# Another table of preferences for the list planner of an attention stage

## The reference

```
s_c = einsum(q, kc);  o_c = softmax(s_c) @ vc        # compressed keys, one for 16 tokens
idx = top_k(score from p_c, 16)                       # blocks of 64 keys to select
o_s = softmax(q @ ks[idx]) @ vs[idx]                  # selected blocks
o_w = softmax(q @ kw, window 512) @ vw                # sliding window
o   = g0 * o_c + g1 * o_s + g2 * o_w
x   = layer_norm(alpha * x + concat(A, o * silu(b_gate)) @ w_out)
```

## Time and profile before

| | |
|---|---|
| median of 3 runs | 1091.5 us (1091.16 to 1092.84) |
| the profiled execution, its own time | 1080.46 us |
| its span, from the first instruction to the last | 1078.6 us |
| TensorE busy, of the span | 96% |
| DVE, ACT, POOL busy, of the span | 70%, 34%, 34% |
| mean granted clock of TensorE | 0.994 of full speed |
| attention on TensorE | 383.8 to 656.8 us |

### The profile page before, as it was taken

The page is one execution under the profiler, slowest core; times in us unless marked ns, Lnnn a source line. Parts: engine busy times, 40 slices in busy tenths (PEclk is TensorE's granted clock), DMA queues, the critical chain, the costliest instruction groups (busy, mean ns, idle before and its releaser), DMA issues.

```text
span 1078.6 us, 19288 instructions
## 1 busy us (share of the span) xinstructions
PE 1034.3 (96%) x7764; PEld 881.2 (82%) x7764; DVE 757.2 (70%) x1397; ACT 371.5 (34%) x785; POOL 369.5 (34%) x384
## 2 busy tenths in 40 slices
PE   6999999999999989999999999999999999999997
PEld 5888999999998965556655666887999999998875
DVE  4577889999898978977678665657546710267755
ACT  3211111122223467878666864111112211253000
POOL 3544540000010498675785562100122211317000
PEclk9999999999999999999999999999999999999999
DMA  8645332144312025040673078312221111042321
GB/s 240 214 166 183 106 115 60 37 163 123 114 40 44 1 90 157 24 137 2 213 258 119 2 238 237 131 64 83 69 88 39 53 44 47 1 156 79 137 83 63
DMA packets 85889, 113.75 MB, mean 105 GB/s; under 512 B 21952, under 2 KB 67144, under 8 KB 85727
## 3 DMA queue, kind: packets, MB, share of 16 engines
q1 hardware_dynamic: 71849, 69.51, 21.2%
q0 software_dynamic: 11776, 41.95, 11.5%
q10 hardware_dynamic: 2182, 1.16, 0.4%
HBM read 100.91 MB, written 16.64 MB: 109 GB/s over the span
## 4 chain that ended last, share of the span: by engine, by line
PE 80%; DVE 6%; POOL 5%; DMA 3%; issue 3%; ACT 1%; SPq 0%; DVEq 0%; POOLq 0%
PE PS L758 25%; PE PS L2165 16%; PE PS L1933 14%; PE PS L1283 4%; PE PS L1395 4%; PE PS L1265 4%; PE PS L746 3%; PE PS L1957 2%; DMA WRAW<-in_w_in_even 2%; POOL RING L1659 2%; PE PS L1946 1%; DVE ACC L597 1%; DMA RING<-in_cache_kv_sel,idx 1%; PE PS L2145 1%; POOL PRW L1674 1%
## 5 line engine op out<-in xcount | busy, mean ns | idle before, releaser
L644 DVE SCALAR_TENSOR_TENSOR Y<-U,SM,Y 128x1024 f32<-128x1024 f32 x120 | 150.1, 1314 | 0.3
L758 PE MATMUL PS<-XH,WH 128*128 128x352 f32 (+1 forms) x624 | 141.3, 330 | 0.0
L758 PE MATMUL PS<-XL,WH 128*128 128x352 f32 (+1 forms) x624 | 138.9, 327 | 0.0
L758 PE MATMUL PS<-XH,WL 128*128 128x352 f32 (+1 forms) x624 | 138.0, 325 | 0.0
L2272 POOL TENSOR_TENSOR WL<-WRAW,WH 128x1024 fp32r<-128x1024 f32 x14 | 37.5, 2675 | 212.8 <-ACT WH L2217 212.8
L758 PEld LDWEIGHTS PS<-XH,WH 128*128 128x128 f32 (+1 forms) x624 | 103.6, 185 | 2.4
L758 PEld LDWEIGHTS PS<-XH,WL 128*128 128x128 f32 (+1 forms) x624 | 104.1, 185 | 1.4
L758 PEld LDWEIGHTS PS<-XL,WH 128*128 128x128 f32 (+1 forms) x624 | 103.8, 185 | 1.4
L597 DVE SCALAR_TENSOR_TENSOR ACC<-PS,SM,ACC 128x508 f32<-128x508 f32 x124 | 86.9, 742 | 25.1 <-PE PS L746 23.1
L2165 PE MATMUL PS<-XH,WH 128*128 128x352 f32 x360 | 77.2, 323 | 0.0
L2165 PE MATMUL PS<-XH,WL 128*128 128x352 f32 x360 | 77.1, 323 | 0.0
(11 more groups left out here) (354 smaller groups left out, 1991.4 us busy)
## 6 DMA issues: line engine op xcount, KB each, us to landing
WRAW<-in_w_in_even SPq DMA_DIRECT2D x16, 512.0 KB, 3.8
WRAW<-in_w_in_odd SPq DMA_DIRECT2D x16, 512.0 KB, 4.0
TM<-in_state_win_kv SPq DMA_DIRECT2D x12, 512.0 KB, 6.8
XIN<-in_x_prompt SPq DMA_DIRECT2D x8, 512.0 KB, 15.6
WRAW<-in_w_in_even SPq DMA_DIRECT2D x16, 256.0 KB, 3.7
XR<-in_x_prompt SPq DMA_DIRECT2D x8, 512.0 KB, 3.5
layer_out<-R SPq DMA_DIRECT2D x8, 512.0 KB, 2.6
XR<-layer_out SPq DMA_DIRECT2D x8, 512.0 KB, 3.3
```

The source lines that it names most:

```text
L644: v.scalar_tensor_tensor(dst, src, CWT[:, i, t:t + 1], dst, ALU.mult, ALU.add).then_inc(s_cv, 1)
L758: ins = pe.matmul(PS[0:mcols, 3 * slot + c, 0:CH], w[:, slot, kk, 0:mcols], x[:, kk, c * CH:(c + 1) * CH], start=(kk == 0 and n == 0), sto ...
```

## The change

Two tables of numbers are replaced. The steps, their lengths, the waits and the rule of choice stay as they are, and so do all instructions; what can differ is the order in which each engine gets its steps, and by it when SP's and POOL's transfers start. The numbers are ns and compare with `remains`, which is at most 193800 and falls to the step's own length at the end of the stage.

```diff
--- before.py
+++ after.py
@@ -1189,13 +1189,12 @@
         assert len(remains) == len(about)
 
 
-        PREFER = {("ACT", "E"): -23000, ("ACT", "P"): 53000, ("ACT", "X"): -28000, ("DVE", "M"): -28000, ("DVE", "O"):
-                  -69000, ("DVE", "P"): 465000, ("DVE", "X"): -164000, ("PE", "D"): 118000, ("PE", "T"): 2000, ("PE", "V"):
-                  -114000, ("PE", "X"): -67000, ("POOL", "C"): 134000}
-        PREFER_EIGHTH = {("ACT", "E", 2): -12000, ("ACT", "E", 3): -31000, ("DVE", "R", 1): 43000, ("PE", "D", 0):
-                  -54000, ("PE", "K", 3): 143000, ("PE", "K", 4): 15000, ("PE", "K", 7): -3000, ("PE", "S", 0): 70000, ("PE", "S",
-                  4): 15000, ("PE", "S", 6): -19000, ("PE", "S", 7): -8000, ("PE", "T", 2): 44000, ("PE", "T", 3): 5000, ("PE",
-                  "T", 4): 17000}
+        PREFER = {("ACT", "E"): 23000, ("ACT", "P"): 176000, ("ACT", "W"): 46000, ("DVE", "H"): -128000, ("DVE", "M"):
+                  -47000, ("DVE", "P"): 601000, ("DVE", "X"): -310000, ("PE", "D"): 113000, ("PE", "K"): -1000, ("PE", "S"):
+                  -39000, ("PE", "V"): -280000, ("PE", "X"): -43000}
+        PREFER_EIGHTH = {("ACT", "E", 1): 68000, ("DVE", "M", 2): -27000, ("DVE", "O", 1): 19000, ("PE", "D", 0):
+                  -115000, ("PE", "K", 1): -108000, ("PE", "K", 3): 112000, ("PE", "K", 4): 19000, ("PE", "S", 0): 109000, ("PE",
+                  "S", 3): -90000, ("PE", "S", 4): 97000, ("PE", "T", 4): 18000, ("PE", "T", 7): -63000}
         order = {e: [] for e in todo}
         now, end, turned_last, pe_mode = dict.fromkeys(todo, 0), {}, [None], WHOLE
         lines = {(e, k): len(todo[e][k]) for e in todo for k in todo[e]}
```

## The result

The changed kernel takes **1096.6 us** (median of 8 runs, 1093.32 to 1099.48) against 1090.81 of the kernel before beside it (8 runs, 1089.71 to 1092.84): ratio 1.0047, interval [1.0033, 1.0062] (5.1 us by the ratio, 5.8 by the medians). The forecast was 1088.5, faster, with a range up to 1095.3. So the sign is wrong and the time lies outside the range. The profiled execution took 1097.15 us, its span is 1095.3 us.

The account below looks back on a forecast made before the run. TensorE bounds the kernel, busy 1034.3 of 1078.6 us, with 17.4 us of gaps in attention. Tail -2.4, clock -1.6 and later scalings +1.0 sum to -3.0: 1088.5 us from 1091.5, 8-in-10 range 1084.8 to 1095.3.

Parts of the forecast that it names:

- Behind attention nothing gives it back: Output projection after attention: 34.4 us of solid matmul cover the second half's weights, so attention's saving reaches the end.
- the 49: Choices, of 1297 along the old order, that the new table changes: 14 ACT, 13 DVE, 11 TensorE, 11 POOL.
- the rivals I set against the forecast: POOL starves the turns 16%, 1095.5; turns beside turns 12%, 1094.1; DMA bounds the tail 27%, 1090.9; orders hardly differ 3%, 1091.5.
- The DMA rival: Transfers fill the DMA engines in attention's tail: landings move only 0.64 us, gap and lower clock stay; 1090.9 us, 27%.
- The sign that I had named for it: Sign of DMA as the tail's bound: the last gather still lands 26 us behind the window loads' issue.
- The tail, -2.4: End of attention: earlier samples' values parts bring gathers forward, cutting 3.07 us of TensorE stalls to 0.7; -2.4 us.
- The clock, -1.6: Near 650 us: without a gap near 2 us TensorE's stay at the lower clock goes; -1.6 us, bounds 0 and 1.6.
- The sign for the tail: Gap ahead of the last values part under 1 us, and no granted clock under 0.95 around it.
- The start, 0: Ten early ACT choices, copies ahead of exponentials: POOL's queue is full, so worth 0; bounds -4.8 to +0.6 us.
- The sign that I had named for the start: The gap of about 3 us on POOL's scaling near 402 is still there.
- The middle, 0: TensorE's swapped turns and key turns: 0, or 2.6 us either way; sign: gaps sum to 4 to 7 us.
- The base: The 11.0 us between profiled 1080.46 and scored median 1091.5, carried over unchanged to turn 1077.5 into 1088.5.

Follow-up runs that it names:

- old_order: The kernel before, unchanged, run again for a second trace on the chip of the first kernels tested: 1090.46 us, ratio 1.0001.
- new_order: The changed kernel, unchanged, measured again beside the kernel before: 1095.2 us, ratio 1.0046.
- new_y_last: The changed kernel with output-projection tiles Y0 and Y1 put back behind the last output turn and V79: 1089.17 us, 0.9984 of the kernel before.
- pv_apart: Changed kernel, Y0 and Y1 behind V79, a values step V between samples' values parts 1 and 2 in both halves: 1088.03 us, 0.9987 of the kernel before.
- y_split: Changed kernel with Y0 ahead of the last output turn and V79, and Y1 behind them: 1087.44 us, 0.9988 of the kernel before, second chip.
- old_y_first: The kernel before with only Y0 and Y1 moved ahead of the last output turn and V79: 1095.88 us, ratio 1.0048.
- the first four experiments: Both kernels unchanged, the changed one with Y0 and Y1 behind V79, the one before with them ahead; one chip: 1090.46, 1095.2, 1089.17, 1095.88 us.
- start_act: The kernel before with only ACT's new preferences for the first 28 of 80 turns, both Y tiles at the end: 1075.79 us, ratio 0.9983.
- the cut at the 54th turn: New table until 54 of 80 turns are placed, old table behind, both Y tiles at the end: 1074.46 us, 0.9963 of the kernel before.

## Why the prediction was wrong

**"Behind attention nothing gives it back"** is the step that failed, and it is worth more than all the others: the whole +5.6. I read 34.4 us of solid matmul in the earlier trace rows as a property of that stretch. It was a property of the order: TensorE was solid there because two tiles stood between the last O and the first weights that wait for O. The planner's code says what would move them. Y waits for the weight step `("wol", 3)`, and behind V79 and O the planner sees nothing: V79 has 1564 ns of work behind it, Y0 has 11080. Run through the planner's loop, the old table ends `wol` 3 at 256.8 us of its own clock, in the moment V79 ends. The new one ends it at 253.0, just before V79's turn at 253.4, so Y wins. It would win under the old preference for V, too (1564 - 114000 is also below 11080). The weights wait for values part 4, which ends 3.5 us earlier by that clock, while TensorE comes to V79's place only 2.6 us earlier. So the earlier samples' parts, which I forecast as the gain, are themselves what let Y pass V79. The planner books that as a success: its last TensorE step ends at 265.6 instead of 268.0, while its last O goes from 257.6 to 266.3. The join behind O is in neither number, as no step of the planner stands there.

**Comparing choices along the old order** hid it. I counted 49 of 1297 choices, and held the rest to be drift. In the end 145 of 333 positions on TensorE differ. Even of the 49 the prediction priced only a part: eight of the eleven on POOL, gathers ahead of the scalings C65 to C77 in the middle, have no term in it. A list scheduler's table can be run in one's head only to the first difference; the rivals I set against the forecast were all of the kind that the 49 suggest, and none has the join. The DMA rival has the tail right, the gap and the lower clock that stay. The sign that I had named for it is there too: the last gather lands 26.6 us behind the window loads' issue (631.94 to 658.53). But that gather was issued only at 650.72, so the sign can't tell full DMA engines from a late issue.

**The tail, -2.4: not found.** The direction of the order was right: parts 0, 1 and 2 come ahead of scores 91 and turn 70, four gathers stand together at 633 to 638, and the stall of part 4 (1.07 in the earlier trace rows) is gone. But `old_order` hasn't got that stall either, so its going isn't shown to be the change's doing. The last one stays:

```profile
655.23 1.08 PE L1282 MATMUL PS<-PT,TM 128*64 128x256 f32 x8
658.53 1.27 PE L1371 MATMUL PS<-RING,PTS 128*32 128x128 f32 x32 [2.22 <-DMA RING<-in_cache_kv_sel,idx]
```

2.22 us here. In the other traces of this tail it is 3.17 (`new_order`), 3.26 (`new_y_last`), 2.61 (`pv_apart`) and 1.51 (`y_split`), against 1.36 in `old_order`, 1.75 in `old_y_first` and 2.00 in the earlier trace rows. POOL's timeline shows where the last gather stands:

```profile
648.81 1.74 POOL L1673 TENSOR_SCALAR PRW<-PRW,STAT,GTOK 128x640 f32<-128x640 f32 x2 [1.94 <-DVE STAT L1513]
650.72 1.00 POOL L1658 DMA_INDIRECT RING<-in_cache_kv_sel,idx  x1 [0.16 <-issue]
```

Parts 1 and 2 had freed the ring when their matmuls ended at 633.76. The last gather is issued 17 us later, behind a scaling that waits 1.94 us for DVE. Whether an earlier issue would have brought it sooner no run shows: the DMA engines were at 0.90 of full use from 645 to 650. I had given POOL's scalings a length (2.38) but no start of their own. From 650.72 to the matmul at 658.53 are 7.8 us, near the 7.1 of the earlier trace rows; the Trainium skill's price for it ("DMA: Bandwidth & Descriptors", "Anatomy of one DMA — SWDGE (gpsimd) path"), an estimate of 3.2 us, is again less than half of what the trace shows.

**The clock, -1.6: not found.** With the stall kept, the fall stays: 0.93 from 640 to 666. And on the chip of the first four experiments there was nothing to win: `old_order` has 1.00 from 650 to 665, while `new_y_last` is at 0.50 from 655.74 to 661.80. The sign for the tail (a gap under 1 us, no clock under 0.95) fails on both counts.

**The start, 0: wrong, by about -1.8.** "POOL's queue is full, so an earlier copy doesn't bring it forward" took POOL's queue as fixed. In `start_act` the copy on ACT lets turn 3 pass scores 8 on TensorE, and POOL's order changes with it: a gather moves in front of the PRC scaling, and the turn is released by PRW. I had the bound (-4.8 to +0.6) and the sign of what hung on it, and took the value 0 because POOL's rows were nearest; `start_act` gives 0.9983. The sign that I had named for the start, "the gap of about 3 us still there", is refuted in the changed kernel:

```profile
403.99 0.71 PE L1264 MATMUL PS<-ident,PRW 64*128 64x64 f32 x16 [1.62 <-POOL PRW L1673]
```

**The middle, 0:** nothing to set against it. Its sign holds: the gaps from 450 to 500 sum to 5.5 us, in the kernel before to 5.4. Waits of turns for DVE's copies are 13.0 us in 19 in the old order and 9.5 in 13 in the new one with Y behind, on one chip.

In sum: start, middle and tail -1.7 (`new_y_last`, 0.9984) instead of -3.0, and the join +6.0 instead of 0. Without the join the predicted sign and about half of its size would have come true, for a reason (the start) other than the one forecast; that would have been luck.

**The base.** I carried 11 us between the profiled 1080.46 and the median of 1091.5 without a row. There is one now, most likely the chip: the kernel before takes 1078.4 us on one chip (26 runs, 1076.13 to 1080.05) and 1090.64 and 1089.62 on two others. Which chip the profile of the earlier trace rows is from isn't on record, but its time fits the first. Set beside the profile of the earlier trace rows instruction by instruction, `old_order` is 0.5 us ahead until some 420, then 0.3 behind to 464 and 1.3 behind from 480 to 520; the distance is 3.8 at 524, 5.9 at 544 and 9.0 at 576, and 9.1 at the end. Carrying the difference over didn't make the miss, which is one of sign, but the trace I argued from lacked the waits that the slower chips have. No kernel but the one before ran on more than one named chip, so that ratios agree across chips isn't shown.

## What the runs showed of the hardware

The same instructions of the same kernel, first on the profile of the earlier trace rows: V's matmuls (L1283), then the copies that wait for them, then the next turn.

```profile
522.23 1.08 PE L1283 MATMUL PS<-PT,TM 128*64 128x256 f32 x8
...
523.42 0.60 ACT L1457 ACTIVATE PT<-PS 128x512 f32<-128x512 f32 x1
523.43 0.69 DVE L1453 COPY PT<-PS 128x512 f32<-128x512 f32 x1 [1.03 <-PE PS L1283]
...
524.42 0.40 PE L1265 MATMUL PS<-ident,PRC 64*63 64x64 f32 x8
```

And in `old_order`, on one of the slower chips:

```profile
523.53 1.08 PE L1283 MATMUL PS<-PT,TM 128*64 128x256 f32 x8
...
527.33 0.60 ACT L1457 ACTIVATE PT<-PS 128x512 f32<-128x512 f32 x1 [2.52 <-remote]
527.34 0.69 DVE L1453 COPY PT<-PS 128x512 f32<-128x512 f32 x1 [3.63 <-remote]
...
528.18 0.44 PE L1265 MATMUL PS<-ident,PRC 64*63 64x64 f32 x8 [2.28 <-DVE PT L1453]
```

The matmuls are recorded alike, ended at 523.31 and 524.61. The copies start 0.1 us later in the one and 2.7 in the other, both engines at once, so it is TensorE's signal that is late and not an engine. It is late right behind the samples' values part 2, in both halves, in every trace from the chips at about 1090 and in that of the changed kernel (2.2 to 4.4 us behind the recorded end of its matmuls). It isn't in the profile of the earlier trace rows, nor in two of the three traces from the chip at 1078; the third has it once, 3.3 us at 630. Nor is part 2 the only place: in `old_order` both copies of the turn behind part 4 start 1.8 us after its recorded end (541.37), where in the profile of the earlier trace rows it is 0.04 us (536.98, 537.02):

```profile
540.66 0.71 PE L1265 MATMUL PS<-ident,PRW 64*128 64x64 f32 x16
...
543.15 0.69 DVE L1453 COPY PT<-PS 128x512 f32<-128x512 f32 x1 [2.63 <-remote]
```

The profile can't assign such a wait and says "remote". The Trainium skill ("Perfetto Trace Analysis", "Summary: the profiler window per engine type") has it that TensorE's window ends at an estimate and leaves out the semaphore's way; this fits that a recorded end proves nothing about the signal, but no run here shows what holds it up.

The second observation is that a gap of 3.49 us in otherwise dense work is followed, 1.5 us after the work resumes, by 3.4 us at a granted clock of 0.50, the level of 1.2 GHz (690.07 to 693.46). In `old_y_first` it is the same (689.88 to 693.28). In `new_order` the clock is at 0.50 already in the gap (from 687.8) and stays there to 694.5, so that the six groups from 689.25 to 694.54 take 5.3 us where six take 2.8. So this stall costs 1.5 to 2.5 us more than the 3.49 it shows.

## What to carry to other kernels

Ask of a solid stretch what makes it solid: find the join inside it, how long the chain from the last input to the first waiting consumer is (9.4 us here), and which movable work lies over it. A scheduler's score is only as good as its last modelled step; work behind the region that waits for its last output has to be in the model, or be pinned. And where a new order loses, move single steps back: one line here turned +0.46% into -0.16%, and the cut at the 54th turn into -0.37%.
